# Attention scores as two packed fp32r products, and page loads shared between two queues

## The chip, the cores and the metric

The kernel runs on one core of a Trainium2 chip. A core has five engines that run side by side and meet at semaphores: TensorE (PE: matrix products from SBUF into PSUM), VectorE (DVE), ScalarE (ACT), GpSimd (POOL) and SyncE (SP), which here only issues DMAs. The metric is the device time of one execution in microseconds.

## The reference

The program is one inference step of a two-layer decoder for a prompt of 1024 tokens and, with the same weights, for 8 samples of one token each. Layer 0 mixes by a short convolution beside attention with a forget gate; layer 1 by a gated linear recurrence; both have an MLP behind them. Only the attention of layer 0 is touched here:

```python
def fox_attend(q, k, v, f_q, f_k, q_pos, k_pos):
    s = jnp.einsum('bqhd,bkhd->bhqk', q, k, preferred_element_type=jnp.float32)
    s = s + jnp.swapaxes(f_q, 1, 2)[..., :, None] - jnp.swapaxes(f_k, 1, 2)[..., None, :]
    s = jnp.where(k_pos[None, :] <= q_pos[:, None], s, -1e30)
    p = jax.nn.softmax(s, axis=-1)
    return jnp.einsum('bhqk,bkhd->bqhd', p.astype(v.dtype), v)
```

The prompt has 8 heads of 64 features and 1024 queries and keys, causal. Each of the 8 samples attends to 2048 cached rows in 16 pages of 128 rows, which stand anywhere in a pool (`cache_k[page_table]`, `cache_v[page_table]`, a page being 128 x 512 fp32, 256 KB), and to its own new row.

## The kernel before

Every engine has a program of its own, written out in order by hand; there is no scheduler. Most of the kernel is dense layers (`product`, `L855`): fp32 operands are split into a high part in fp32r and a low rest, and three fp32r products (high-high, high-low, low-high) of 128 x 128 weights by 344 columns are summed. The attention stage, from some 383 to 720 us in the trace of before, stands between the first layer's input projection and its output projection.

The stage is a loop over h = 0 to 7 (`head`, one for each engine), in which head h of the prompt is weighted and normed, head g = h + 1 is prepared, and sample h attends to its cached pages. For head g TensorE turns keys and queries from token rows to feature rows (`keys_turned`, `queries_turned`), ScalarE copies them from PSUM to `kT[g % 2]` and `qT[g % 2]` (`keys_kept`, `queries_kept`), and `scores` computes the scores with queries as rows, in 12 pieces of 128 queries by 128 to 512 keys. VectorE takes the maximum of each piece (`peak_of`), and then makes each query's shift (`shift`). For head h TensorE turns the shift into rows of `qT` (`shift_turned`, 16 small products, `L1123`, the first thing of a head), computes the scores again with keys as rows, in 12 pieces (`scores_turned`, `L1136`), ScalarE takes their exponents into `PT` (`exponent`, `L1582`), and `weighted` (`L1151`) multiplies these by the values. Score products are fp32: 64 features plus a row for the cumulated log forget value of the key (`negF`), and with keys as rows one more for the shift (`QS`). A piece on the diagonal gets a bf16 product of 128 columns that adds the mask.

A piece of 512 columns is a PSUM bank. `scores` go round three banks (`RING`), so piece p waits for the maximum of piece p - 3; `scores_turned` use two banks, so piece p waits for exponent p - 2. In TensorE's order, value product p stands behind score piece p + 1 and behind the score pieces of the next head given by `scores_at` (two each at p = 2 to 6, one at 7 and 8). ScalarE's order in a head is: two copies of the shift rows, the softmax denominator of head h - 1, two copies of keys, exponent 0, two copies of queries, exponents 1 to 11.

Sample h's cached keys come by pairs of pages, eight pairs, into seven slots (`kpages`, `L582`), are multiplied by the query on GpSimd (`L778`, `keys_multiplied`, for sample h + 1 during head h) and reduced on VectorE (`L1985`, `key_scores`). The values come into eight slots (`vpages`), and TensorE multiplies them by the sample's weights at the end of the head (`sequence_values`, `L1178`). All of these loads are issued by SyncE, in `load_pages`: for each page it reads the page's number from the table on the chip (`pt`) into a register, checks its bounds, and issues a DMA. SyncE's order is, for each h: eight pairs of keys, each when its slot is free, then the eight pairs of values of sample h + 1.

## Time and profile before

| | |
|---|---|
| runs of before | 2924.05, 2926.5, 2928.64 us; median 2926.5 |
| the profiled execution | 2922.55 us, of which the traced span is 2920.7 |
| TensorE busy | 2813.4 us, 96% of the span, granted clock 0.987 of full on average |
| VectorE, GpSimd, ScalarE busy | 1307.9, 883.9, 530.9 us |
| chain that ended last | 90% on TensorE; 69% in the dense layers' line 855 |
| lines of the attention's fp32 products | L1111, L1136 and L1151, 2% each of the chain; 74.1, 81.7 and 83.0 us busy |
| cached pages | 2 x 128 DMAs of 256 KB, median 3.0 to 3.1 us from issue to landing |

The busy time of an engine is the union of its instructions' spans; a matrix product's record includes its way through the array, so the distance between starts and not the duration of one says what it costs in a row of them. An fp32 product appears as two records. The chain follows the work back from the last instruction through what released each step. A stage lasts as long as its chain; an engine with gaps in the stage can still hold the others up at one place in it.

### The profile page before, as it was taken

What the parts mean: (1) busy time and instruction counts of PE and PEld (TensorE: products, weight loads), DVE (VectorE), ACT (ScalarE), POOL (GpSimd) and SP (SyncE); (2) the same over time, 40 slices, a digit from 0 to 9 for tenths busy, and PEclk for the clock granted to TensorE, in tenths of its full rate; (3) what the DMA queues carried; (4) which work ended last, traced back from release to release, by engine and by line L of the source; (5) the groups of instructions that cost most, each with busy time, mean ns of one, the idle gap of its engine ahead of it and who ended that gap; (6) DMA issues with size and microseconds to landing.
All of it is one profiled execution on the core that took longest, in us unless ns stands there. A gap on an engine that the chain in (4) does not pass through costs nothing.

```text
span 2920.7 us, 42681 instructions
## 1 busy us (share of the span) xinstructions
PE 2813.4 (96%) x16931; PEld 2498.8 (86%) x16931; DVE 1307.9 (45%) x2088; ACT 530.9 (18%) x829; POOL 883.9 (30%) x490
## 2 busy tenths in 40 slices
PE   5999989999999999999999999999899999999998
PEld 3899954445899999999999899954899999999998
DVE  3116755554354343444356303156454444434445
ACT  4200012323041010100101413134241010010100
POOL 2322235443222322333323322200324333243330
PEclk9999999999999999999999999999999999999999
DMA  7411267775512322223211322141301111111111
GB/s 313 123 44 37 59 202 234 217 213 152 210 37 101 101 73 90 84 82 107 66 37 44 103 63 103 51 147 55 118 30 56 45 44 46 41 50 38 55 43 58
DMA packets 208126, 275.37 MB, mean 94 GB/s; under 512 B 10742, under 2 KB 152713, under 8 KB 201068
## 3 DMA queue, kind: packets, MB, share of 16 engines
q1 hardware_dynamic: 204812, 255.89, 27.6%
q10 hardware_dynamic: 3024, 16.88, 1.5%
q8 instruction: 107, 1.75, 0.3%
q0 software_dynamic: 144, 0.52, 0.0%
q14 instruction: 39, 0.32, 0.0%
HBM read 245.24 MB, written 28.04 MB: 94 GB/s over the span
## 4 chain that ended last, share of the span: by engine, by line
PE 90%; DVE 4%; issue 2%; ACT 2%; SPq 1%; DMA 1%; POOL 0%; DVEq 0%; ACTq 0%
PE ps L855 69%; PE ps L873 4%; PE ps L841 2%; PE ps L1151 2%; PE ps L1136 2%; PE ps L1111 2%; PE ps L997 1%; PE ps L1178 1%; DVE xT L1856 1%; PE ps L1305 1%; PE ps L904 1%; PE ps L1294 1%; PE ps L1333 1%; PE ps L1312 1%; DMA ada_late<-in_w_ada_dram 1%
## 5 line engine op out<-in xcount | busy, mean ns | idle before, releaser
L756 POOL CAST whi<-stage 128x1024 fp32r<-128x1024 f32 x194 | 207.9, 1072 | 1770.5 <-PE ps L855 1298.5
L855 PE MATMUL ps<-hh,whi 128*128 128x344 f32 x2832 | 607.7, 323 | 5.7 <-issue 2.0
L855 PE MATMUL ps<-hl,whi 128*128 128x344 f32 x2832 | 601.6, 321 | 0.0
L855 PE MATMUL ps<-hh,wlo 128*128 128x344 f32 x2832 | 598.0, 319 | 0.0
L757 POOL TENSOR_TENSOR wlo<-stage,whi 128x1024 fp32r<-128x1024 f32 x194 | 519.4, 2677 | 15.5
L855 PEld LDWEIGHTS ps<-hh,whi 128*128 128x128 f32 x2832 | 474.4, 188 | 26.1 <-issue 24.6
L855 PEld LDWEIGHTS ps<-hl,whi 128*128 128x128 f32 x2832 | 479.5, 189 | 0.0
L855 PEld LDWEIGHTS ps<-hh,wlo 128*128 128x128 f32 x2832 | 472.1, 188 | 0.0
L855 PE MATMUL ps<-hid_hi,whi 128*128 128x344 f32 x1536 | 330.4, 323 | 10.7 <-DVE xT L1856 10.7
L855 PE MATMUL ps<-hid_lo,whi 128*128 128x344 f32 x1536 | 326.6, 321 | 0.0
L855 PE MATMUL ps<-hid_hi,wlo 128*128 128x344 f32 x1536 | 324.8, 320 | 0.0
L1877 DVE TENSOR_TENSOR tmp<-tmp 128x1032 f32<-128x1032 f32 x64 | 81.3, 1271 | 532.3 <-ACT tmp L1496 532.3
L855 PEld LDWEIGHTS ps<-hid_hi,whi 128*128 128x128 f32 x1536 | 254.9, 188 | 27.0 <-DVE xT L1856 17.0
L1496 ACT ACTIVATE tmp<-ps 128x1032 f32<-128x1032 f32 x64 | 66.2, 1034 | 1150.6 <-PE ps L855 1142.6
L855 PEld LDWEIGHTS ps<-hid_lo,whi 128*128 128x128 f32 x1536 | 258.0, 188 | 0.0
L855 PEld LDWEIGHTS ps<-hid_hi,wlo 128*128 128x128 f32 x1536 | 257.7, 189 | 0.0
L1856 DVE SCALAR_TENSOR_TENSOR xT<-ps,modT,xT 128x688 f32<-128x688 f32 x269 | 248.4, 924 | 0.0
L1842 DVE TENSOR_TENSOR t<-ps,modT 128x8 f32<-128x8 f32 x272 | 45.1, 166 | 347.9 <-PE ps L855 320.3
L778 POOL TENSOR_TENSOR kpages<-kpages,qbc 128x1024 f32<-128x1024 f32 x60 | 140.5, 2372 | 141.9 <-DMA kpages<-in_cache_k_dram 140.8
L1844 DVE SCALAR_TENSOR_TENSOR xT<-ps,modT,xT 128x336 f32<-128x336 f32 x272 | 152.1, 559 | 0.1
L1882 DVE TENSOR_TENSOR hid_lo<-tmp,hid_hi 128x1032 fp32r<-128x1032 f32 x64 | 106.6, 1665 | 41.9 <-ACT hid_hi L1498 38.6
L1843 DVE TENSOR_TENSOR xT<-xT,t 128x8 f32<-128x8 f32 x272 | 102.6, 377 | 9.3
(331 smaller groups left out, 2477.7 us busy)
## 6 DMA issues: line engine op xcount, KB each, us to landing
stage<-in_w_ff_dram SPq DMA_DIRECT2D x128, 512.0 KB, 3.9
kpages<-in_cache_k_dram SPq DMA_DIRECT2D x128, 256.0 KB, 3.1
vpages<-in_cache_v_dram SPq DMA_DIRECT2D x128, 256.0 KB, 3.0
ada_late<-in_w_ada_dram SPq DMA_DIRECT2D x32, 1024.0 KB, 5.2
stage<-in_w_in_even_dram SPq DMA_DIRECT2D x25, 512.0 KB, 3.9
stage<-in_w_in_odd_dram SPq DMA_DIRECT2D x25, 512.0 KB, 3.9
xstore<-xT ACTq DMA_DIRECT2D x2, 4128.0 KB, 12.6
xT<-xstore SPq DMA_DIRECT2D x2, 4128.0 KB, 12.5
```

Of the source, the lines that this page charges most:

```text
L756: link(pool.tensor_copy(whi[:, u.c % 4, :], stage[:, u.c % 2, :]))
L757: pool.tensor_tensor(wlo[:, u.c % 4, :], stage[:, u.c % 2, :], whi[:, u.c % 4, :].bitcast(F32), ALU.subtract).then_inc(w_split, 1)
L778: pool.tensor_tensor(kk, kk, qbc[:, b % 2, :].unsqueeze(1).to_broadcast([P, 2, 512]), ALU.mult).then_inc(k_mul, 1)
L841: return pe.transpose(out, in_, ident[0:k, 0:k])
L855: last = pe.matmul(ps[:, 3 * t.par + c, 0:CH], w, x[:, c * CH:(c + 1) * CH], start=(k == 0 and q == 0), stop=(k == n - 1 and q == 2))
L873: return pe.matmul(ps[:, 3 * ((t.c + j) % 2) + c, 0:CH], w, x[:, k, c * CH:(c + 1) * CH], start=(k == 0 and first), stop=(k == KT - 1 and ...
L1496: act.activation(thirds(tmp[:, j, :]), acc(tt.par), ACT.Relu).then_inc(acc_free[tt.par], 1)
L1843: tt(xT[:, f, 0:NS], xT[:, f, 0:NS], t8[:, :], ALU.add)
L1844: first = stt(out=xT[:, f, NS:CH], in0=ps[:, s, NS:CH], scalar=modT[:, l, m, NS:NC], in1=xT[:, f, NS:CH], op0=ALU.mult, op1=ALU.add)
L1856: stt(out=x2, in0=ps[:, s + 1:s + 3, 0:CH], scalar=modT[:, l, m, NS:NC], in1=x2, op0=ALU.mult, op1=ALU.add).then_inc(acc_free[t.par], 1)
L1877: tt(tmp[:, j, :], tmp[:, j, :], tmp[:, j, :], ALU.mult).then_inc(hid_squared, 1)
L1882: tt(hid[1][:, i.c % 2, j, :], tmp[:, j, :], hid[0][:, i.c % 2, j, :].bitcast(F32), ALU.subtract).then_inc(hid_ready, 1)
```

## The change

Four things, all in the attention stage.

1. Scores. `qT` and `kT` hold fp32r values, each the rounded high part, and there are four more buffers: `qhl` with the query's high part in rows 0 to 63 and its low rest in rows 64 to 127, and `klh` with the key's low rest in rows 0 to 63 and its high part in rows 64 to 127. A score piece is two fp32r products: high by high (with the rows for forget value and shift, each now as a high and a low row) and, over 128 rows at once, high by low plus low by high. The high parts in the new buffers are copied by ScalarE from `kT` and `qT` (four more copies a head), the low rests are made by VectorE from PSUM (`key_lows`, `query_lows`), and TensorE waits for both.
2. `PT` is a ring of three pieces instead of room for a head's 12, so exponent n waits for value product n - 3.
3. The two page numbers of a pair are read by one instruction, and not checked; instead VectorE clamps the page table once.
4. The cached values of samples 1 to 7 are issued by ScalarE, a pair each behind exponents 1 to 8. The semaphore `xt_done` also counts the low parts.

```diff
-        PT = at("PT", [P, NB * (NB + 1) // 2 * P], F32, B0)
-        qT = [at(f"qT{i}", [HD + 2, SEQ], F32, B0 + 18432 + 4096 * i) for i in range(2)]
-        kT = [at("kT0", [HD + 2, SEQ], F32, B0 + 26624), at("kT1", [HD + 2, SEQ], F32, W0 + 8192 + 4096 * KSLOTS)]
+        PT = at("PT", [P, 3, 512], F32, B0)
+        qT = [at(f"qT{i}", [HD + 4, SEQ], F32R, o) for i, o in enumerate((W0 + 4096, B0 + 6144))]
+        kT = [at(f"kT{i}", [HD + 4, SEQ], F32R, o) for i, o in enumerate((B0 + 10240, W0 + 8192 + 4096 * KSLOTS))]
+        qhl = [at(f"qhl{i}", [P, SEQ], F32R, B0 + 14336 + 4096 * i) for i in range(2)]
+        klh = [at(f"klh{i}", [P, SEQ], F32R, B0 + 22528 + 4096 * i) for i in range(2)]
...
             def load_pages(cache, slot, n, sem):
 
-                for q in range(2):
-                    page = sp.value_load(pt[0:1, 2 * n + q:2 * n + q + 1], min_val=0, max_val=cache_k.shape[0] - 1)
+                _, pages = nc.values_load_multi_w_load_instructions(
+                    pt[0:1, 2 * n:2 * n + 2], engines=[mybir.EngineType.SP], min_val=0, max_val=cache_k.shape[0] - 1,
+                    skip_runtime_bounds_check_because="the page table's copy on the chip is clamped to the cache's pages")
+                for q, page in enumerate(pages):
                     sp.dma_start(slot[:, q, :], cache[ds(page, 1), 0].rearrange("a p h d -> (a p) (h d)")).then_inc(sem, 16)
...
-                for j in range(8):
-                    load_values(h + 1, j)
+            sp.wait_ge(a_st, NP * (NH - 1))
             load_unit(V(U_OUT[0]), woe[:, :, 0:P])
...
             def queries_turned(g, c):
                 if c == 0 and g:
                     pe.wait_ge(a_q2, 2 * g)
                 if c == 1:
-                    pe.wait_ge(a_k, 2 * g + 1)
+                    pe.wait_ge(a_k, 4 * g + 1)
+                    pe.wait_ge(xt_done_or_lows, lows(4 * g + 1))
...
                 o = ps[:, RING[(4 + p) % 3], 0:w]
-                last = pe.matmul(o, qT[g % 2][0:HD + 1, i * P:(i + 1) * P], kT[g % 2][0:HD + 1, lo:lo + w],
-                                 start=True, stop=not diag)
+                pe.matmul(o, qT[g % 2][0:HD + 2, i * P:(i + 1) * P], kT[g % 2][0:HD + 2, lo:lo + w], start=True, stop=False)
+                last = pe.matmul(o, qhl[g % 2][:, i * P:(i + 1) * P], klh[g % 2][:, lo:lo + w], start=False, stop=not diag)
...
-                last = pe.matmul(o, kT[h % 2][0:HD + 2, j * P:(j + 1) * P], qT[h % 2][0:HD + 2, lo:lo + w],
-                                 start=True, stop=not diag)
+                pe.matmul(o, kT[h % 2][0:HD + 4, j * P:(j + 1) * P], qT[h % 2][0:HD + 4, lo:lo + w], start=True, stop=False)
+                last = pe.matmul(o, klh[h % 2][:, j * P:(j + 1) * P], qhl[h % 2][:, lo:lo + w], start=False, stop=not diag)
...
+                act.activation(kT[g % 2][0:HD + 2, cols], ps[0:HD + 2, RING[c], :], ACT.Copy).then_inc(a_k, 1)
+                act.wait_ge(a_k, 4 * g + 2 * c + 1)
+                act.activation(klh[g % 2][HD:P, cols], kT[g % 2][0:HD, cols].bitcast(F32), ACT.Copy).then_inc(a_k, 1)
...
-                o = key_at[j] + lo - j * P
-                act.activation(PT[:, o:o + w], ps[:, 4 + p % 2, 0:w], ACT.Exp).then_inc(a_p, 1)
+                n = NP * h + p
+                if n >= 3:
+                    act.wait_ge(a_av, n - 2)
+                act.activation(PT[:, n % 3, 0:w], ps[:, 4 + p % 2, 0:w], ACT.Exp).then_inc(a_p, 1)
+
+            def load_values(b, j):
+                act.wait_ge(v_used, 4 * (b - 1) + j // 2 + 1)
+                n = 8 * b + j
+                _, pages = nc.values_load_multi_w_load_instructions(
...
+                for q, page in enumerate(pages):
+                    act.dma_start(vpages[:, j, q, :], cache_v[ds(page, 1), 0].rearrange("a p h d -> (a p) (h d)")
+                                  ).then_inc(first_or_values[j], 16)
...
                 for p in range(1, NP):
                     exponent(h, p)
+                    if h and p <= 8:
+                        load_values(h, p - 1)
...
+                link(dve.tensor_scalar(QS[:, :, 2], peak[:, :], -1.0, None, ALU.mult))
+                stt(out=QS[:, :, 3], in0=peak[:, :], scalar=-1.0, in1=QS[:, :, 2].bitcast(F32), op0=ALU.mult, op1=ALU.subtract
+                    ).then_inc(a_shift, 1)
+
+            def key_lows(g, c):
+                dve.wait_ge(a_k, 4 * g + 2 * c + 1)
+                cols = slice(512 * c, 512 * c + 512)
+                tt(klh[g % 2][0:HD, cols], ps[0:HD, RING[c], :], kT[g % 2][0:HD, cols].bitcast(F32), ALU.subtract
+                   ).then_inc(xt_done_or_lows, 1)
...
                 if more:
                     key_scores(8 * g)
+                    for c in range(2):
+                        key_lows(g, c)
+                    for c in range(2):
+                        query_lows(g, c)
                 sequence_top(h)
```

ScalarE near a head's start, before: from the shift rows of head 1 to exponent 2 (`qT`, `kT` are the operands in SBUF, `rden` the denominators, `PT` the exponents).

```order
L1575 ACTIVATE qT_140<-ps 2x512 [waits a_again] x2
L1592 ACTIVATE rden<-ps 64x512 [waits a_av]
L1594 ACTIVATE rden<-rden 64x512 [waits a_lnd]
L1567 ACTIVATE kT_141<-ps 65x512 [waits a_tk] x2
L1582 ACTIVATE PT<-ps 128x512 [waits a_st]
L1571 ACTIVATE qT_139<-ps 64x512 [waits a_tq] x2
L1582 ACTIVATE PT<-ps 128x512 [waits a_st]
L1582 ACTIVATE PT<-ps 128x384 [waits a_st]
```

The same place in the changed kernel, from the second copy of keys to the first pair of value pages.

```order
L1574 ACTIVATE klh_146<-kT_142 64x512 [waits a_k]
L1594 ACTIVATE PT<-ps 128x512 [waits a_av,a_st]
L1579 ACTIVATE qT_140<-ps 64x512 [waits a_tq]
L1581 ACTIVATE qhl_144<-qT_140 64x512 [waits a_q]
L1579 ACTIVATE qT_140<-ps 64x512 [waits a_tq]
L1581 ACTIVATE qhl_144<-qT_140 64x512 [waits a_q]
L1594 ACTIVATE PT<-ps 128x512 [waits a_av,a_st]
L1599 TENSOR_LOAD pt [waits v_used]
L1603 ISA
L1603 DMA vpages<-in_cache_v_dram 128x512
```

Each copy to `kT` and `qT` has a second, dependent copy behind it, ahead of exponents 0 and 1, and behind exponent 1 stand the load of page numbers and the DMAs.

TensorE in the middle of a head, before: score pieces of head h (`L1136`) and h + 1 (`L1111`), masks (`L1139`, `L1114`), a value product (`L1151`).

```order
L1136 MATMUL ps<-qT_139,kT_141 128x512 [waits a_p]
L1111 MATMUL ps<-kT_142,qT_140 128x512 [waits a_max]
L1111 MATMUL ps<-kT_142,qT_140 128x128 [waits a_max]
L1114 MATMUL ps<-negb,identb 128x128
L1151 MATMUL ps<-PT,Vp 128x256 [waits a_p]
```

The same place now.

```order
L1142 MATMUL ps<-qT_139,kT_141 128x512 [waits a_p]
L1143 MATMUL ps<-qhl_143,klh_145 128x512
L1117 MATMUL ps<-kT_142,qT_140 128x512 [waits a_max]
L1118 MATMUL ps<-klh_146,qhl_144 128x512
L1117 MATMUL ps<-kT_142,qT_140 128x128 [waits a_max]
L1118 MATMUL ps<-klh_146,qhl_144 128x128
L1120 MATMUL ps<-negb,identb 128x128
L1157 MATMUL ps<-PT,Vp 128x256 [waits a_p]
```

The order of pieces and their waits is the same; a piece is two instructions instead of one (which the trace shows as two records for fp32).

VectorE at the start of the same head, now (`small` and `peaks` are the maxima of sample and prompt).

```order
L2010 TENSOR_REDUCE sc<-kpages 128x16 [waits k_mul]
L2182 TENSOR_TENSOR klh_146<-ps,kT_142 64x512 [waits a_k] x2
L2188 TENSOR_TENSOR qhl_144<-ps,qT_140 64x512 [waits a_q] x2
L2136 TENSOR_REDUCE small<-ps 8x1 [waits d_tops_turned]
L2137 TENSOR_SCALAR small<-ident,small 8x8 [waits dve_link]
L2168 TENSOR_REDUCE peaks<-ps 128x1 [waits a_s] x2
```

The four instructions in rows two and three are new; the others stood in this order before.

## Rows read from the trace of the kernel before

**Rows 1.** Window: length, busy (count) of PE, PEld, DVE, ACT, POOL; clock, DMA share, GB/s.
```profile
470.00:510.00 40.00, 39.20 (x183) 18.69 (x181) 20.65 (x36) 11.64 (x23) 19.57 (x9) 1.00 0.81 235
```

**Rows 2.** Chain of waits: start us, duration us, engine, tile, line, count.
```profile
450.09 1.84 PE ps L1123 x16
...
490.55 1.84 PE ps L1123 x16
...
498.60 0.59 ACT kT L1567
...
501.39 1.07 ACT qT L1571 x2
...
503.09 1.10 PE ps L1151 x2
...
515.41 0.12 PE ps L1169 x2
...
522.70 0.91 PE ps L1151 x2
...
531.00 1.07 PE ps L1123 x9
...
692.84 1.84 PE ps L1123 x16
...
718.44 0.02 issue
```

**Rows 3.** Chain, score pieces of 512, 384, 256 and 128 columns.
```profile
504.30 0.86 PE ps L1136 x2
...
480.57 0.65 PE ps L1136 x2
...
483.15 0.43 PE ps L1136 x2
...
472.35 0.22 PE ps L1136 x2
```

**Rows 4.** Window of line 855 alone (fp32r, 344 columns): PE and PEld busy (count).
```profile
1000.00:1010.00 10.00, 9.09 (x58) 8.81 (x57) 1.00 0.26 77
```

**Rows 5.** Timeline of ScalarE: start us, us, engine, line, operation, tiles.
```profile
493.03 0.59 ACT L1592 ACTIVATE rden<-ps 64x512 f32<-64x512 f32 x1
493.65 0.63 ACT L1594 ACTIVATE rden<-rden 64x512 f32<-64x512 f32 x1
```

**Rows 6.** VectorE: a window; then by line busy, mean ns | idle before; one timeline row.
```profile
504.33:523.43 19.10, 19.10 (x68) 9.98 (x67) 15.59 (x24) 5.00 (x10) 10.03 (x5) 1.00 0.82 236
...
L2140 DVE TENSOR_REDUCE peaks<-ps 128x1 f32<-128x512 f32 (+3 forms) x12 | 6.5, 554 | 3.4 <-PE ps L1111 2.1 <-PE ps L1114 1.3
L1985 DVE TENSOR_REDUCE sc<-kpages 128x16 f32<-128x1024 f32 x5 | 6.0, 1209 | 0.0
L2108 DVE TENSOR_REDUCE small<-ps 8x1 f32<-8x128 f32 x1 | 0.3, 279 | 7.8 <-PE ps L841 7.8
...
523.67 2.34 DVE L2147 TENSOR_SCALAR QS<-peak 128x8 f32<-128x8 f32 x1
```

**Rows 7.** Queues of SyncE and ScalarE: issue, a timeline row, then by line min/median/max ns.
```profile
490.52 17.78 SPq L582 DMA_DIRECT2D vpages<-in_cache_v_dram  x16
...
L581 SPq TENSOR_LOAD <-pt x53: 262/268/279, 479.9 to 543.9; - x53
L582 SPq DMA_DIRECT2D vpages<-in_cache_v_dram x28: 332/333/1016, 490.5 to 544.6; - x28
L611 SPq DMA_DIRECT2D out_dram<-in_state_conv_dram x1: 5601/5601/5601, 415.2 to 415.2; - x1
...
L1667 ACTq DMA_DIRECT2D rstore<-qe x4: 343/352/382, 1737.6 to 1811.7; - x4
```

**Rows 8.** Window with stores and page loads together, columns as in rows 1.
```profile
410.00:415.00 5.00, 5.00 (x27) 2.20 (x24) 0.38 (x1) 1.18 (x2) 0.00 (x0) 0.85 1.02 377
```

**Rows 9.** Timeline of TensorE, the shift of head 0, with the wait ahead of it.
```profile
408.57 3.31 PE L1123 MATMUL ps<-ident,QS 128*2 128x128 f32 x16 [7.31 <-DVE QS L2147]
```

More of the change, by code:

```diff
@@ L162, in build @@
         lft = put("lft", [P, NB + 1, NH])
-        negF = put("negF", [P, NB, NH])
-        QS = put("QS", [P, NB, 2])
+        negF = put("negF", [P, NB, NH, 2], F32R)
+        QS = put("QS", [P, NB, 4], F32R)
         prevT = put("prevT", [P, 4, 16])
@@ L448, in multiplied, with lows @@
             return n // 2 + 1 if n < PAGES // 2 else n - 3
-        key_at = [sum(SEQ - m * P for m in range(j)) for j in range(NB)]
+        def lows(n):
+            return KT + n
         def all_read(eng, t):
@@ L603, in _ @@
             for j in range(8):
-                load_values(0, j)
+                load_first_values(j)
             sp.wait_ge(qk_scaled, 2 * NB)
@@ L990, in _ @@
                                 xin[:, b, k * P:(k + 1) * P])
-                last.then_inc(xt_done, 1)
+                last.then_inc(xt_done_or_lows, 1)
             pe.wait_ge(setup_dve, 3)
@@ L1085, in keys_turned @@
                     turn(o[0:HD, :], QK[:, 1, b, g * HD:(g + 1) * HD])
-                    last = pe.matmul(o[HD:HD + 1, :], negF[:, b, g:g + 1], ident[:, :], start=True, stop=True)
+                    last = pe.matmul(o[HD:HD + 2, :], negF[:, b, g, :].bitcast(F32), ident[:, :], start=True, stop=True)
                 last.then_inc(a_tk, 1)
@@ L1580, in exponent @@
                 act.wait_ge(a_st, NP * h + p + 1)
-                o = key_at[j] + lo - j * P
-                act.activation(PT[:, o:o + w], ps[:, 4 + p % 2, 0:w], ACT.Exp).then_inc(a_p, 1)
+                n = NP * h + p
[6 more added lines that the diff above has]
+                _, pages = nc.values_load_multi_w_load_instructions(
+                    pt[0:1, 2 * n:2 * n + 2], engines=[mybir.EngineType.Activation], min_val=0, max_val=cache_k.shape[0] - 1,
+                    skip_runtime_bounds_check_because="the page table's copy on the chip is clamped to the cache's pages")
+                for q, page in enumerate(pages):
+                    act.dma_start(vpages[:, j, q, :], cache_v[ds(page, 1), 0].rearrange("a p h d -> (a p) (h d)")
+                                  ).then_inc(first_or_values[j], 16)
             def denominator(h, c):
@@ L2188, in head @@
                 sequence_masked(h)
+            for c in range(2):
+                key_lows(0, c)
+            for c in range(2):
+                query_lows(0, c)
             dve.wait_ge(prep_pe, PE_STEP["u_turned"])
```

54 lines of the change are left out of this document (31 added, 23 removed).

## Prediction

> **What bounds the kernel now.** I read the windows of the attention stage first, then the chain of waits through one head, then the durations by line, and last the queues of SyncE and ScalarE. The windows show TensorE busy 39.2 of 40 us at the full clock, while VectorE is busy 20.7, ScalarE 11.6 and GpSimd 19.6 [rows 1]. The chain gives the period of a head as the distance between two shift products (`L1123`): 490.55 - 450.09 = 40.46 us. Head 7 starts at 692.84, so heads 1 to 6 take (692.84 - 450.09) / 6 = 40.46 us each; head 0 starts at 408.57 [rows 9] and takes 41.5, the last head, which prepares no other, ends at 718.44 and takes 25.6 [rows 2]. Inside a head the chain is TensorE, except near its start, where it passes twice through ScalarE: a copy of keys and then an exponent (from 498.60), and two copies of queries and then an exponent (from 501.39), after which the second value product starts at 503.09 [rows 2]. So what shortens the score products shortens the head, as long as neither ScalarE's two passages nor VectorE takes over.
>
> **The score products.** Each fp32 score product stands as two MATMUL records: a piece of 512 columns takes 0.86 us, of 384 0.65, of 256 0.43, of 128 0.22 [rows 3]. The new form is two fp32r products per piece. The trace has none of 512 columns, but 58 of 344 columns fill 9.09 us, 0.157 us each [rows 4]. In proportion to columns, a product of 512 takes 0.233 us and a pair 0.47, say 0.46 as part of the 0.157 will not grow. I save 0.40 us on a piece of 512, 0.30 on 384, 0.19 on 256. For 128 columns the two ends are 2 x 0.058 = 0.12 us in proportion, and 2 x 0.157 = 0.31 if loading the 128 weights is the floor; the row that is nearest, the fp32 pair at 0.22, makes me take 0.17. The ends for all sizes: no gain at all (a product as long as an fp32 record, 0.43) and 0.42 per large piece. A head has 12 pieces of queries and 12 of keys, each set six of 512 and two each of 384, 256 and 128: 12 x 0.40 + 4 x 0.30 + 4 x 0.19 + 4 x 0.05 = 6.96 us of TensorE time per head.
> By the Trainium skill's page TensorE: Matmul & The Clock Gate (Back-to-back issue gap), a product of N columns takes N/2.4 ns and some 2.5 ns; a product of 344 would be 0.146 us where the row has 0.157, and a pair of 512 would be 0.43 us, 0.03 below my value and 0.4 us more gain per head. The measured row decides.
>
> **ScalarE's copies at the head's start.** This takes a part back. Key copies: the second key copy starts 0.02 us after TensorE, takes 0.59, and exponent 0 starts 0.49 after it (independent instructions overlap by 0.1: two query copies fill 1.07 instead of 2 x 0.59). Now a second copy of the same block waits for the first to end and lies ahead of exponent 0. Two dependent ScalarE instructions of this size start 0.62 us apart [rows 5]. The keys come 0.40 earlier (the first score piece), the exponent 0.62 later: the first value product starts 0.2 us later than before, and the second score piece's gain is lost in that wait. Query copies: two independent ones take 1.07 us; now copy, dependent copy, copy, dependent copy: exponent 1 starts 0.62 + 0.49 + 0.62 + 0.49 = 2.22 us after the first copy's start rather than 2 x 0.49 = 0.98, +1.25. The second value product starts (before at 503.09) 0.2 + 1.3 = 1.5 us later, at 504.6. VectorE's low parts (four of 64 x 512, 0.7 us each if they go by columns like the peaks, 0.554 for 384 in the mean) stand where it sits idle for 7.8 us [rows 6]; the wait of query turns for the first of them is met, as it follows one key reduction (1.21) and the first copy is done 2 us before. They cost nothing unless the key reduction ahead of them is late.
>
> **The rest of a head.** From 503.09 to 531.00 TensorE spent 27.91 us. Nine score pieces of keys (4 x 0.40 + 0.30 + 2 x 0.19 + 2 x 0.05 = 2.38) and the 12 of queries (3.48) take 5.86 off: 22.05. VectorE now comes close. From 504.33 to 523.43 it did 15.6 us of work, with 3.4 idle for score pieces [rows 6]; TensorE's share of that stretch falls from 19.1 by 2.2 (keys) and 3.5 to 13.4. TensorE came to the spread of the sums (`L1169`) 12.3 us after the start of its second value product [rows 2]; less 1.0 (four key pieces) and 2.0 (eight of queries) that is 9.3. VectorE starts 504.33 - 503.09 = 1.24 later and has until the sums two top instructions (0.9), six peaks of 0.554 (3.3), three key reductions of 1.21 (3.6), shifting and sums (0.65): 9.7. The difference is 0.4 us; with the way through the semaphores I add 0.5. After that TensorE's waits for free banks are met, and the sequence's weights are ready about when the first cached values are multiplied. The shift (`L2147`, 2.34 us here) gets a second small instruction; between the last peak and the next head lie eight products and the cached values, over 5 us [rows 2, 6]. Head: 504.6 + 22.05 + 0.5 = 527.1, from 490.55 that is 36.6 us, 3.9 less.
>
> **Pages.** On SyncE a page takes 17.78 / 16 = 1.11 us of issue: a load of 0.27, a DMA of 0.33, and register steps, a check and gaps between [rows 7]. Sixteen value and sixteen key pages are 35.5 us of the 40.46, so SyncE itself would have been near the bound at 36.6; that is what moving the values away buys, and it needs no gain of its own. A pair now is one load, and two DMAs each with a register step, without the check: some 0.30 + 2 x 0.52 = 1.34 us (an estimate from that 1.11: load and check were 0.59 of it). ScalarE's own DMAs elsewhere take 0.34 to 0.38 us of issue [rows 7]. Eight pairs, 10.7 us per head, stand in ScalarE's order behind exponents 1 to 8. Behind each waits the next exponent, for which the next value product waits. From exponent 1 to 8 TensorE needed 19.6 us (503.09 to 522.70, second to ninth value product [rows 2]), now 19.6 - 5.7 + 0.5 = 14.4: seven steps of 2.06 us, against 1.4 for dispatching an exponent and a pair: hidden, with 0.6 us to spare. Even if the load waited for the running exponent (0.60) it would be 1.94. In the last head a step of TensorE is only some 1.3 us, so there ScalarE leads with 8 x 1.4 us, and of the 3.5 us that the products save 0.8 remain. The value slots were freed a head earlier, so that wait costs nothing.
> The values then come in 14 us, together with five pairs of keys: 13 x 0.524 MB = 6.8 MB. The engines moved 377 GB/s between 410 and 415 us, and 235 at a share of 0.81 in heads (290 at full) [rows 1, 8]. At 377 this is 18 us and the last pair is there 1 to 2 us before its product; at 290 it is 23.5, some 4.5 us too late. I take 377, since the 235 were set by the issue of 1.11 us per page.
> The Trainium skill's page DMA: Bandwidth & Descriptors (Issuing engines are not separate DMA queues) says that DMAs of several engines share the same 16 and only the issuing time is saved; its page Perfetto Trace Analysis (DMA Instruction, HWDGE) has a lock on the descriptor generator that the queues share, so that each of ScalarE's DMAs might wait for one of SyncE's. No row here shows two queues issuing densely together. By that rule, with the 0.33 us of a row for each wait, a step would be 1.4 + 2 x 0.33 = 2.06 us, just what TensorE leaves; past it lies rival (1).
>
> **Outside heads 1 to 6.** Before head 0 the scores start 1.5 us later for ScalarE's four added copies, VectorE gets back 1 to 1.5 of the gaps it had between peaks, and TensorE's wait of 7.3 us for the shift stays [rows 9]: 0, with +1.5 as an end. Head 0 has no value pages on ScalarE; it saves 3.9 and, as keys are issued in 1.34 instead of 2.2 us, some of the 1.1 us by which it was longer: 4.5. The clamp of the page table, the second negF and the ring of three PT buffers (a product three pieces back) are 0.2 to 0.4 us beside other work: 0.
> Sum: 6 x 3.9 + 4.5 + 0.8 = 28.7, of which I take 28. The profiled execution took 2922.55 us (span 2920.7), the median is 4 above it; 2922.5 - 28 = 2894.5 there, 2898.5 as the median.
>
> **Rivals.** (1) Slower: ScalarE's queue leads. Place: the two DMA issues between exponents 1 and 8. For it: on SyncE the same instruction took up to 1.02 us in this stage, and 5.6 behind the stores of 2 MB each [rows 7]. Against: its median is 0.33. It decides from a step of 2.06 us, and makes the head longer than before from (14.4 + 3.9) / 7 = 2.6 us, that is 0.93 us per DMA. At 1.02 each, a step is 2.75: heads of 41.6 (+1.1 x 6), the last +8, less 4.5 for head 0: 2937. (2) Values land late: at 290 GB/s a head is 36.6 + 4.5 = 41.1, and all but head 0's gain is gone: 2925 to 2930, no change. (3) VectorE or ScalarE bind more than I see (a small instruction as long as `L2147`'s 2.34 us in a worse place; low parts behind a late key page): 2 us more in seven heads, 2912. (4) Nothing takes back: 7 x 7 + 3.5 + 1 = 53 us, 2873. (5) fp32r pairs of full fp32 length: the copies remain, 7 x 1.9 - 1 more, 2938; 58 products at 0.157 speak against.
>
> **Chances.** Forecast 0.64 (2882 to 2912), (3) 0.13, (4) 0.05, (2) 0.06, (1) 0.10, (5) 0.02. The range 2878 to 2925 takes in the forecast, (3), the milder half of (2) and leaves out about 0.2. What differs by less than 0.2% (5.9 us) can't be told from no change. Faster: 0.64 + 0.12 + 0.05 + 0.01 = 0.82; same 0.06; slower 0.12.
>
> **What would show it.** Distance between shift products 36 to 37 us instead of 40.46; a pair of 512 columns at 0.46; the start of the second value product 14 us after the shift; TensorE waiting some 2 us there and 0.5 at the sums; ScalarE's DMAs at 0.33 to 0.4 us each; no wait for value pages at `L1178`. I am wrong if the heads stay at 40 us: then the cached values' product waits for DMA (2) or value products wait for exponents at every piece (1).

## The result and the profile after

The changed kernel took 2917.7 us (median of 19 runs, 2907.3 to 2930.0) beside 2927.1 for the kernel before (19 runs, 2923.2 to 2934.4): a ratio of 0.9966, 95% interval 0.9955 to 0.9977. It is faster, by 9.4 us, where 28 were forecast. Its times spread over 23 us; those of before over 11.

Its first profiled execution is the longest of the 19, 2930.0 us; a second one took 2905.4, below all 19. The two stand at both ends of what one program does, and most of what separates them (23.5 of 24.6 us) lies in heads 1 to 6. No profile shows an execution near the median. The window of heads 1 to 6 of either, first the long one (columns as in [rows 1]; clock, DMA share and GB/s last):

```profile
449.08:701.92 252.84, 227.50 (x1099) 118.91 (x1098) 148.43 (x243) 86.14 (x162) 103.69 (x47) 0.87 0.59 198
```

```profile
449.19:678.57 229.38, 204.45 (x1099) 110.84 (x1098) 148.21 (x243) 86.16 (x162) 103.67 (x46) 0.98 0.65 219
```

Before, six heads took 242.75 us at clock 1.00 [rows 1, 2]. TensorE was busy 39.20 of 40 us then; now it is busy 204 of 229, and the mean granted clock is 0.98 or 0.87: of its two levels it was at 1.2 GHz for about 2 x 0.13 = 26% of the long window (66 us) and 4% of the short one (9 us). The chain of waits of the long profile, with the starts of heads 1, 2, 3, 4, 6 and 7 and the DMAs between them (start, length, what), answers to [rows 2]:

```profile
449.15 1.84 PE ps L1129 x16
...
491.33 3.51 PE ps L1129 x16
...
525.68 8.35 DMA vpages<-in_cache_v_dram
...
536.21 1.84 PE ps L1129 x16
...
565.18 8.77 DMA vpages<-in_cache_v_dram
...
576.12 1.84 PE ps L1129 x16
...
658.37 3.51 PE ps L1129 x16
...
701.99 1.85 PE ps L1129 x16
```

Heads last 42.2, 44.9, 39.9, 40.3, 41.9 and 43.6 us instead of 40.46. Two things are new in the chain: loads of value pages ahead of a head's end, and two shifts, those of heads 2 and 6, whose 16 products took 3.51 us where they took 1.84 [rows 2], which is the same work at 1.2 GHz. Both lie in a long stretch at 1.2 GHz that starts inside a wait for value pages. The first (columns as above):

```profile
486.50:510.50 24.00, 22.04 (x74) 9.24 (x75) 4.44 (x7) 6.32 (x11) 17.18 (x8) 0.50 0.16 58
```

TensorE waited 2.74 us for pages there, until 487.55. The second starts in a wait of 2.52 us and runs from 654 to 677. The two make some 48 of the 66 us.

The short profile shows the head without disturbance. Head 2 of it, TensorE's timeline (start, length, line, shapes; in brackets the idle time and its releaser), down to the next head's shift:

```profile
488.25 1.91 PE L1129 MATMUL ps<-ident,QS 128*4 128x128 f32 x16
...
498.01 1.10 PE L1157 MATMUL ps<-PT,Vp 128*128 128x512 f32 x2 [1.38 <-ACT PT L1594]
...
502.61 1.10 PE L1157 MATMUL ps<-PT,Vp 128*128 128x512 f32 x2 [2.20 <-ACT PT L1594]
...
508.71 0.40 PE L1117 MATMUL ps<-kT,qT 66*128 66x512 f32 x1
508.94 0.40 PE L1118 MATMUL ps<-klh,qhl 128*128 128x512 f32 x1
509.18 0.22 PE L1117 MATMUL ps<-kT,qT 66*128 66x128 f32 x1
...
510.13 0.48 PE L1117 MATMUL ps<-kT,qT 66*128 66x512 f32 x1
510.45 0.39 PE L1118 MATMUL ps<-klh,qhl 128*128 128x512 f32 x1
510.68 0.28 PE L1117 MATMUL ps<-kT,qT 66*128 66x256 f32 x1
...
523.60 1.06 PE L1182 MATMUL ps<-vpages,PBx 128*32 128x512 f32 x8 [0.41 <-DMA vpages<-in_cache_v_dram]
...
525.57 0.60 PE L1129 MATMUL ps<-ident,QS 128*4 128x128 f32 x4
```

A pair of 512 columns fills 509.18 - 508.71 = 0.47 us behind another fp32r product and 0.55 behind a diagonal's bf16 product (0.32 to the second, not 0.23), against 0.86 [rows 3]. TensorE waits 1.38 and 2.20 us for exponents 0 and 1, and 0.41 for the last value pages. ScalarE in the same head (ACTq is its queue), answering to [rows 5, 7]:

```profile
500.21 0.63 ACT L1581 ACTIVATE qhl<-qT 64x512 fp32r<-64x512 f32 x1
...
501.89 0.57 ACT L1594 ACTIVATE PT<-ps 128x512 f32<-128x512 f32 x1
502.10 0.83 ACTq L1603 DMA_DIRECT2D vpages<-in_cache_v_dram  x2
503.04 0.49 ACT L1594 ACTIVATE PT<-ps 128x384 f32<-128x384 f32 x1 [0.58 <-issue]
503.71 0.84 ACTq L1603 DMA_DIRECT2D vpages<-in_cache_v_dram  x2
...
515.20 0.88 ACTq L1603 DMA_DIRECT2D vpages<-in_cache_v_dram  x2
```

And what the loads' instructions took over six heads (min/median/max ns), with the time from issue to landing in us:

```profile
L1599 ACTq TENSOR_LOAD <-pt x48: 486/497/689, 463.1 to 691.5; - x48
```

```profile
L1603 ACTq DMA_DIRECT2D vpages<-in_cache_v_dram x96: 339/340/827, 464.0 to 692.7; - x96
...
DMA to landing us min/median/max: 2.6/4.2/10.1
```

A DMA's issue costs what was forecast (0.34 us); the load of the page numbers takes 0.50 where 0.30 was. The eight pairs are issued from 502.1 to 516.1, the last of them lands at 523.5, and TensorE was there at 523.2. From the first issue to that landing the engines moved 320 GB/s, and in the first 4 us, while pages are issued one pair in 1.6 us, 160:

```profile
502.10:523.50 21.40, 20.58 (x107) 11.75 (x107) 19.03 (x29) 6.48 (x14) 11.13 (x6) 1.00 0.90 320
...
502.00:506.00 4.00, 3.39 (x18) 2.39 (x18) 2.08 (x6) 1.55 (x3) 2.54 (x2) 1.00 0.57 160
```

The DMA stretch 475 to 490 of the same profile (DMA busy tenths, GB/s, then queue SP and queue ACT with packets, MB and share):

```profile
DMA  9999999999999999999999999978995979499951
GB/s 415 404 399 399 366 361 388 404 388 415 344 344 371 377 366 393 393 399 404 393 393 404 388 399 377 213 126 284 393 437 202 218 158 213 175 388 393 339 197 55
...
q1 hardware_dynamic: 1725, 3.14, 62.0%
q10 hardware_dynamic: 1053, 1.90, 33.9%
```

Both queues together move some 390 GB/s while they are full, here the first 9 us of the 15.

### The profile page after: what moved, and what is told of

It reads as the page before. It is cut to its first block, busy times and chain, and to the rows that moved or that the text cites. A ratio compares the mean times of both kernels' runs of the same rounds, so it can differ in the third digit from the quotient of the medians.

```text
span 2928.3 us, 42220 instructions
## 1 busy us (share of the span) xinstructions
PE 2793.0 (95%) x16931; PEld 2504.5 (86%) x16931; DVE 1327.9 (45%) x2130; ACT 551.9 (19%) x861; POOL 882.6 (30%) x490
## 4 chain that ended last, share of the span: by engine, by line
PE 88%; DVE 5%; ACT 2%; DMA 2%; issue 2%; ACTq 0%; SPq 0%; DVEq 0%
PE ps L859 68%; PE ps L877 4%; PE ps L845 3%; PE ps L1157 2%; DMA vpages<-in_cache_v_dram 2%; PE ps L1001 1%; DVE xT L1880 1%; PE ps L1090 1%; PE ps L1309 1%; PE ps L908 1%; PE ps L1337 1%; PE ps L1298 1%; PE ps L1129 1%; PE ps L1316 1%; PE ps L1182 1%
## 5 line engine op out<-in xcount | busy, mean ns | idle before, releaser
L1906 DVE TENSOR_TENSOR hid_lo<-tmp,hid_hi 128x1032 fp32r<-128x1032 f32 x64 | 106.5, 1664 | 41.9 <-ACT hid_hi L1502 38.6
L1157 PE MATMUL ps<-PT,Vp 128*128 128x512 f32 (+3 forms) x192 | 88.6, 544 | 24.7 <-ACT PT L1594 24.1
```

Source lines behind the costliest of these rows:

```text
L1157: last = pe.matmul(ps[:, 2 + c, lo - 512 * c:512], Vp[:, j, odd:odd + 2, :].rearrange("p e d -> p (e d)"), PT[:, (NP * h + p) % 3, 0:w], s ...
L1906: tt(hid[1][:, i.c % 2, j, :], tmp[:, j, :], hid[0][:, i.c % 2, j, :].bitcast(F32), ALU.subtract).then_inc(hid_ready, 1)
```

## The experiments

The theories, as the expectations name them. L: value pages land late, and the clock falls from that wait. I: their issue holds ScalarE up. K: the clock falls without them, in the pauses that the shorter products leave. C: ScalarE's order at the head's start makes these pauses. K2, K's second form: the clock falls because TensorE stands in these pauses. P: VectorE and GpSimd share a port. "Behind the heads" is from the end of the last sequence's product to the end of the span. Each run is compared with the kernel before on the same chip (2926.8 to 2928.4 there).

**Without the value pages of samples 1 to 7.** Those samples are weighted with stale pages.

```diff
-                    if h and p <= 8:
-                        load_values(h, p - 1)
-                    pe.wait_ge(first_or_values[j], 16 + 32 * (b + 1))
+                    pe.wait_ge(first_or_values[j], 16 + 32)
```

> The changed kernel without the value pages of samples 1 to 7: ScalarE issues none of them and TensorE waits only for the first sample's (samples 1 to 7 are weighted with stale pages). Theory L (late landing: TensorE stands at the value products of a head, and the clock falls to 1.2 GHz from that): heads 1 to 6 take 36 to 37 us each instead of 39.9 to 44.9, the granted clock stays at 1.0 in them as in head 0, and the time is 25 to 32 us under the kernel before, some 2897. Rival I (the cost is the pages' issue on ScalarE): the same time, since the issue is gone too. Rival K (the shorter packed products alone leave TensorE too idle, and the clock falls with no page waited for): heads stay at 39 us or more with stretches at 1.2 GHz, and the time stays within 15 us of the kernel before.

2905.4 us, ratio 0.9927 (0.9913 to 0.9940). Heads 37.8 to 39.6 us. Its window of heads 1 to 6:

```profile
450.78:682.28 231.50, 211.42 (x1100) 115.58 (x1100) 144.51 (x244) 85.55 (x162) 103.46 (x46) 0.94 0.35 108
```

That is between the forecasts of L (2897) and K (within 15 us of the kernel before). L alone is refuted: no page is waited for and the clock is still at 0.94. In head 3, from 528.53, it falls behind the two waits for exponents 0 and 1:

```profile
528.53:542.60 14.07, 10.78 (x67) 5.95 (x66) 6.21 (x11) 8.11 (x14) 7.03 (x3) 1.00 0.46 132
542.70:546.00 3.30, 3.12 (x7) 1.72 (x7) 0.50 (x2) 0.41 (x2) 0.00 (x0) 0.50 0.00 0
```

Every head of this run has such a stretch, 10 to 15 us after its start. K holds for a part.

**A sixteenth of the bytes.** The issues stay, each page's first 32 of 512 columns are moved.

```diff
-                    act.dma_start(vpages[:, j, q, :], cache_v[...].rearrange("a p h d -> (a p) (h d)")
+                    act.dma_start(vpages[:, j, q, 0:32], cache_v[...].rearrange("a p h d -> (a p) (h d)")[:, 0:32]
```

> The changed kernel with every value page issued as before by ScalarE in its place, but only 32 of the page's 512 columns moved (samples 1 to 7; a sixteenth of the bytes; the rest of the tile is stale). Theory L (the bytes land late): the pages land within 2 to 3 us of their issue, nothing waits at the value products, heads 36.5 to 37.5 us at clock 1.0, the time 22 to 30 us under the kernel before. Rival I (the issue delays ScalarE's exponents, and TensorE behind them): as the changed kernel as it stands, heads of 40 us or more, 10 us under the kernel before. Rival K (clock without waits): the same as in the run without values, short of L.

2907.4 us, ratio 0.9930 (0.9916 to 0.9943). So bytes cost 10.3 of the changed kernel's time. The issue makes 2 us more than the run without pages, which the intervals can't part: in the profiles the last head is 4.1 us longer with it (29.2 and 25.1), but heads 1 to 6 are 3.3 shorter and what lies behind the heads 5.0. Heads 1 to 6:

```profile
451.20:679.45 228.25, 209.99 (x1099) 114.36 (x1098) 146.60 (x244) 86.27 (x162) 103.34 (x47) 0.95 0.40 116
```

**SyncE issues the values again**, by pairs, behind the key pages.

```diff
+                for j in range(8):
+                    load_values(h + 1, j)      # SyncE
-                    if h and p <= 8:
-                        load_values(h, p - 1)  # ScalarE
```

> The changed kernel with the value pages issued by SyncE again, behind the key pages of the same head and by pairs; the packed scores stay. SyncE has 32 pages in a head; at the 17.8 us that 16 pages took before less half of the register loads it issues them in about 31 us of a 36.6 us head. Theory L: what matters is when they are issued; keys come first on the queue, so the values of a head are issued no earlier than with ScalarE, and it is 0 to 15 us slower than the changed kernel, about 2917 to 2930. Rival I: ScalarE is free of the issue, heads get to 37 us and the time falls to 2900 or under.

2908.3 us, ratio 0.9934 (0.9921 to 0.9948): between the two ranges (I 2900 or under, L 2917 or over). I had the order wrong: SyncE has issued the next head's keys by the end of a head, and sends the values in the first 12 us of a head, not in its second half. All of them land in time:

```profile
448.91:679.94 231.03, 211.46 (x1099) 115.54 (x1099) 144.48 (x243) 85.57 (x162) 103.62 (x46) 0.94 0.66 217
```

217 GB/s here and 108 without the values, in the same time: bytes that come early cost nothing.

**Value pages earlier on ScalarE.**

```diff
+                    load_values(h, 4)          # behind the second denominator
...
+                if h:                          # behind exponent 0
+                    load_values(h, 5)
+                    load_values(h, 6)
...
-                    if h and p <= 8:
-                        load_values(h, p - 1)
+                    if h and p == 1:
+                        load_values(h, 7)
...
+                if more:                       # behind exponent 11
+                    for j in range(4):
+                        load_values(g, j)
```

> The changed kernel with the same value pages issued by ScalarE earlier: pairs 0 to 3 of the next sample behind the last exponent piece of a head (ScalarE idles 5 us there), pair 4 behind the second denominator, 5 and 6 behind the first exponent piece of the next head, 7 behind its second. Theory L: all land 8 us or more before their product, no wait there and clock 1.0; heads of 36.5 to 37.5 us, the time 22 to 30 us under the kernel before, some 2900. Rival I: the issue costs ScalarE as much wherever it stands, and earlier it stands ahead of the key and query copies that TensorE waits for: no better than the changed kernel, 2915 to 2925. Rival K: clock falls anyway, no gain over the changed kernel of more than 5 us.

2917.6 us, ratio 0.9971 (0.9961 to 0.9982): as the changed kernel. No page was waited for, but the four pairs at a head's end hold ScalarE until the slots are free and beyond. TensorE waits for the shift's copy 1.5 us in head 1 and 0.2 to 0.5 in four others, and the mean clock of heads 1 to 6 is 0.93. The time is in rival I's range (2915 to 2925), and in K's (no gain over 5 us); the trace shows rival I's place, but whether that is all of it stays open. ScalarE, then TensorE:

```profile
443.19 6.43 ACTq L1603 DMA_DIRECT2D vpages<-in_cache_v_dram  x8
449.67 1.07 ACT L1585 ACTIVATE qT<-ps 4x512 fp32r<-4x512 f32 x2 [7.07 <-PE ps L1129]
```

```profile
450.31 0.50 PE L1142 MATMUL ps<-qT,kT 68*128 68x512 f32 x1 [1.46 <-ACT qT L1585]
```

**The page changes alone**, on the kernel before.

```diff
+                _, pages = nc.values_load_multi_w_load_instructions(pt[0:1, 2 * n:2 * n + 2], ...)
...
-                for j in range(8):
-                    load_values(h + 1, j)      # SyncE
...
+                    if h and p <= 8:
+                        load_values(h, p - 1)  # ScalarE
                 last = pe.matmul(o, qT[g % 2][0:HD + 1, ...], kT[g % 2][0:HD + 1, ...])   # fp32, as before
```

> The kernel before (fp32 scores, its large tile for the exponents) with the page changes alone: page numbers by pairs, and samples 1 to 7's value pages issued by ScalarE behind its exponent pieces 1 to 8. The issue stands about 4 us earlier against the value products than in the changed kernel, since heads take 40.46 us and not 36. Theory L (late landing decides): the last pages land before their product, heads stay at 40.5 us, same time as before within 3 us. Rival I (the issue on ScalarE costs): exponents run late by 0.3 us or more eight times in a head, heads 41 to 43 us, 5 to 20 us slower than before.

2922.9 us, ratio 0.9982 (0.9973 to 0.9991), and not the 5 to 20 us slower of rival I. Heads 1 to 6 are the old ones to 0.01 us, at full clock:

```profile
453.27:696.03 242.76, 237.98 (x1100) 114.15 (x1099) 125.20 (x210) 70.60 (x138) 102.68 (x47) 1.00 0.61 204
```

The other stages of its profile are not the same: head 0 takes 45.3 us instead of 41.5 (TensorE waits 2.0 for VectorE's product of 6.85 us beside ten GpSimd products, and the clock is at 0.91 instead of 0.97), the last head 28.8 instead of 27.5, with ScalarE's issue in it, and what lies behind the heads is 3.6 us shorter. SyncE is done with pages earlier and sends the modulation weights of the next layer part sooner: in the kernel before TensorE waited for them 3.7 us (the profiles' line L997, here of before), in the changed one 1.4.

```profile
  DMA ada_late<-in_w_ada_dram: 3.7, 2
```

**TensorE's pauses filled**, with SyncE's values: work that nobody reads, in place of waiting.

```diff
+                if p < 2:
+                    for i in range((6, 9)[p]):
+                        pe.matmul(ps[:, 2 + c, 0:P], ident[:, :], ident[:, :], start=True, stop=True)
                 pe.wait_ge(a_p, NP * h + p + 1)
```

> The run with SyncE's values, with TensorE's waits for exponent pieces 0 and 1 filled: 6 and 9 products of the identity with itself (fp32, 128 columns, 0.22 us each, 1.3 and 1.9 us) into the accumulator that the piece's own product then starts anew. It tells the clock from the waits: the waits stay as long, only TensorE's activity changes. Theory K2 (the clock falls because TensorE stands there): no stretch at 1.2 GHz in heads 1 to 6, each head 36.0 to 36.6 us instead of 37.7 to 39.6, time 2893 to 2900. Rival (the clock falls for something else): stretches stay, time 2908 to 2912 (each filler ends 0 to 0.3 us late).

2898.7 us, ratio 0.9902 (0.9888 to 0.9916), 9.6 under the run with SyncE's values, though TensorE does more. Heads 36.51 to 36.55 us:

```profile
448.40:667.61 219.21, 218.97 (x1280) 129.37 (x1279) 142.20 (x243) 85.56 (x162) 103.62 (x46) 1.00 0.70 229
```

That is K's second form shown: nothing but TensorE's activity in the pauses is different, and the clock stays at 2.4 GHz. Over heads 1 to 6 that is 11.8 us (231.0 to 219.2); the last head, where nothing was to be gained, is 2.4 longer.

**The same fillers in the changed kernel**, ScalarE issuing the values (edit as above).

> The changed kernel as it stands, ScalarE issuing the values, with the same 6 and 9 filler products in TensorE's two waits for exponents 0 and 1. With the changed kernel (2917.7), the run with SyncE's values (2908.3) and that with SyncE's values and fillers (2898.7) it closes the square. If late pages and the pauses at a head's start act apart: 2917.7 - 9.6, 2908 within 3. If the late pages alone let the clock fall (their waits stand behind 20 us of work): 2914 or more. If the pauses at a head's start are what the page waits need to let it fall: 2902 or under.

2916.7 us, ratio 0.9956 (0.9943 to 0.9970): not told from the changed kernel. Heads 1 to 6 took 233.2 us at clock 0.98, with 7.6 us of waits for value pages:

```profile
448.00:681.23 233.23, 225.23 (x1280) 130.63 (x1279) 143.91 (x243) 86.13 (x162) 104.27 (x47) 0.98 0.63 215
```

```profile
  DMA vpages<-in_cache_v_dram: 7.6, 5
```

Of the three forecasts that is the second (2914 or more): the page waits let the clock fall by themselves. It is at 1.2 GHz from some 37 us after the start of head 1, and from 38 after that of head 5, for 7 and 3 us, across the next head's start, and nowhere else in heads 1 to 6. Late pages take back what the clock gives: the two losses don't add. How much of this run's time is something else stays open, as its profile is also 6.6 us longer behind the heads than the long profile of the changed kernel.

**Exponents 0 and 1 earlier.** Theory C, with ScalarE's values.

```diff
+                exponent(h, 0)
                 if more:
                     keys_kept(g, 0)
                     keys_kept(g, 1)
-                exponent(h, 0)
+                exponent(h, 1)
...
-                    exponent(h, p)
+                    if p > 1:
+                        exponent(h, p)
```

> The changed kernel with exponent pieces 0 and 1 of a head moved in ScalarE's order: piece 0 ahead of the four key copies, piece 1 ahead of the four query copies, where ScalarE idles 1.8 and 1.7 us (run without values). Theory C (TensorE's two waits of 1.4 and 2.2 us for these pieces are ScalarE's order, and the clock falls behind them): both waits go, up to 3.5 us a head, and with them most stretches at 1.2 GHz; but the value pages are issued where they were and are needed 3 us earlier, so part comes back at the value products: 2895 to 2912. Rival (the copies themselves bind: what goes at the exponents comes back at the scores' wait for the query copies): no change against the changed kernel, 2917 within 4.

2912.6 us, ratio 0.9956 (0.9942 to 0.9969): between C's range and the rival's, and its interval overlaps with the changed kernel's, so by the time alone it settles nothing. The waits for exponents 0 and 1 fell from 3.6 to between 0.5 and 1.0 us, and a wait for value pages of 1.6 to 3.3 us took their place in five of six heads, 12.4 us in all. Head 0 has a new wait too, 5.5 us for VectorE, as in the next run:

```profile
  DMA vpages<-in_cache_v_dram: 12.4, 5
```

**The same, with SyncE's values.**

> The same new places of exponent pieces 0 and 1, and the value pages issued by SyncE as in the run with SyncE's values (2908.25). Theory C: heads 1 to 6 lose the two waits (3.5 us) and one stretch at 1.2 GHz (1.7 us of a stretch of 3.4): 33 to 35 us instead of 37.7 to 39.6, so 8 heads by 4 us: 2876 to 2888. Rival (copies bind): 2904 to 2910. Rival K (TensorE's own idle share lets the clock fall in any case): half of it, 2890 to 2900.

2884.5 us, ratio 0.9851 (0.9837 to 0.9865). Heads of 33.2 and 34.3 us in turn, at full clock:

```profile
453.49:655.88 202.39, 198.90 (x1099) 107.67 (x1099) 150.28 (x240) 85.24 (x162) 103.22 (x46) 1.00 0.75 244
```

The copies don't bind; their place ahead of two exponents did. Only head 0 got longer, 43.0 us, with 5.4 of waiting for VectorE and the clock at 0.86. TensorE, then VectorE in head 0 and in head 1, then GpSimd:

```profile
445.20 1.94 PE L1186 MATMUL ps<-vpages,PBx 128*32 128x512 f32 x8 [5.43 <-DVE PBx L2157]
```

```profile
437.08 8.06 DVE L2157 TENSOR_TENSOR PBx<-PBx,small 128x136 f32<-128x136 f32 x1
...
477.83 0.30 DVE L2157 TENSOR_TENSOR PBx<-PBx,small 128x136 f32<-128x136 f32 x1
```

```profile
419.40 25.59 POOL L786 TENSOR_TENSOR kpages<-kpages,qbc 128x1024 f32<-128x1024 f32 x11 [21.67 <-DMA kpages<-in_cache_k_dram]
```

VectorE's product ends at 445.14, 0.15 us behind the end of GpSimd's block (444.99). So it does in the two other runs with a long block: 443.20 and 443.04 with ScalarE's values and the new order, 445.43 and 445.27 with the page changes alone.

**Key pages 10 to 14 ahead of the stores.**

```diff
+            for n in range(KSLOTS + 3, KSLOTS + 8):
+                load_keys(n)
             sp.wait_ge(qk_scaled, 2 * NB)
             ...                                # nine stores
-            for n in range(KSLOTS + 3, KSLOTS + 8):
-                load_keys(n)
```

> The run with SyncE's values and the two exponents moved, with the key pages 10 to 14 issued by SyncE ahead of the nine stores at the start of head 0 and not behind them. There head 0 took 43.0 us, with a wait of 5.4 us for VectorE's product for the weights of the first sample (128x136, two SBUF inputs), which took 8.06 us beside 11 key products of GpSimd without a pause and 0.30 us in other heads. Theory P (a port that the two engines share: VectorE's product starts only when GpSimd pauses): GpSimd begins its key products some 10 us earlier and has no block of 11; the product takes 0.3 to 2.3 us, head 0 takes 36 to 38 us, time 2877 to 2880. Rival (the DMA's keys set it, not the port): GpSimd's block only starts earlier or stays, head 0 within 2 us of 43.0, time 2884.

2882.5 us, ratio 0.9847 (0.9833 to 0.9860). GpSimd works in shorter blocks, VectorE's product takes 1.92 us, and head 0 takes 34.2 at a clock of 0.94:

```profile
440.48 1.92 DVE L2157 TENSOR_TENSOR PBx<-PBx,small 128x136 f32<-128x136 f32 x1
```

The place and the product's time are as the port theory has them; head 0 is shorter than its 36 to 38 us, 8.8 less than above where the wait was 5.4, with the clock higher too. But head 0 starts 4.6 us later (415.1 instead of 410.5), so 4 us stay in the profiles and 2.0 in the medians, less than the two intervals can part, and the time misses the 2877 to 2880 expected. A shared port is the explanation that fits; no run rules out another.

**The last sample's pages split** between the queues, on top of that.

```diff
-                for j in range(8):
+                for j in range(8 if h < NH - 2 else 4):
                     load_values(h + 1, j)      # SyncE
+                    if h == NH - 1 and p in (1, 2, 3, 4):
+                        load_values_act(h, p + 3)      # ScalarE
```

> The run above, with the value pages of the last sample split: pairs 0 to 3 by SyncE, 4 to 7 by ScalarE behind its exponent pieces 1 to 4 of the last head, which has no key or query copies. SyncE gets to the output projection's weights and the late modulation weights 6 us earlier: theory: the wait of 1.9 us for a late modulation weight after the heads, and the stretch of 3.4 us at 1.2 GHz behind it, go (they are absent in the changed kernel): 3 to 4 us less than the run above. Rival: the four pairs on ScalarE hold up its exponents or land late in the last head: the same or up to 3 us slower than the run above.

2878.5 us, ratio 0.9831 (0.9817 to 0.9844), the fastest: 49.9 us under the kernel before and 39 under the changed one. It is 4.0 us under the run above, as expected, though the intervals overlap. The wait for modulation weights behind the heads is down to 0.4 us, from 3.5.

**The changed kernel once more.**

> The changed kernel unaltered, profiled once more, since its first profiled execution (2930.0 us) was the longest of 19 and 12 us over their median of 2917.7. Theory L with the clock: the value pages are issued and land at the same places (15 to 28 us into a head, 8 to 10 us each at the end), TensorE waits for them in most heads, but less time is at 1.2 GHz: heads of 38 to 41 us, the profiled execution within 6 us of 2917.7. If the first profile shows the rule and not the tail, heads are 40 to 45 us again.

2914.5 us (5 runs), ratio 0.9951 (0.9932 to 0.9971), and the profile shown above. Heads of 37.3 to 39.3 us, shorter than I expected, and an execution 12.3 us under 2917.7 where I expected one within 6: the first profile was one tail, this is the other.

## Why the prediction was wrong

The direction was right and the mechanism of the gain was right to a few tenths; the time was 19 us too low, because one term was mis-sized and one missing.

- **Score products.** A pair was taken at 0.46 and measures 0.47 to 0.55. The stretch from the second value product to the next shift was put at 527.1 - 504.6 = 22.5 us; it is 22.55 without page waits (525.57 - 502.61 - 0.41). Right.
- **ScalarE's copies.** The second value product was forecast 14.05 us after the shift and comes at 14.36 (502.61 - 488.25). Right within 0.3. I counted what this costs in time and stopped there; that it makes two pauses of 1.4 and 2.2 us in an engine that had one of 0.6 was the start of the second failure.
- **A head of 36.6 us** is what remains once pages are early and the clock is kept: 36.5 in the run with fillers. That this run's 2898.7 us is the forecast of 2898.5 is in part luck: its profile is only 21.7 us under that of before, since its head 0 starts 2.7 us later and 3.3 more go by behind the heads, where I had nothing, and the last head gains nothing; the rest of the 28 is that the profile of before was 4.5 under its median and this one 2.2 over. VectorE's 0.5 at the sums shows as 0.50 us of waiting of TensorE's weight load, with the products ahead of it still running; rival (3) did not happen.
- **Step that failed first: the pages' bytes.** "At 377 this is 18 us and the last pair is there 1 to 2 us before its product ... I take 377." The bytes were right (6.84 MB in head 2 of the short profile), the rate over the whole stretch was not: the engines reach 350 to 395 GB/s only once pages have piled up, and from the first issue to the last landing it is 320 and 21.4 us. That is 3.4 us more than 18, where the margin was 1 to 2. The pages are issued from 13.9 us into the head, share the engines with key pages (12 of those beside the 16 value pages), and the last ones take 7.8 us there and up to 10.1 in the long profile. They come 0.4 to 1.2 us late in the short profile and up to 2.7 in the long one. Rival (2) was the right place with the wrong size. Removing the bytes gives back 10.3 us, earlier issue by SyncE 9.4.
- **Step that was missing: TensorE's clock.** Before, heads ran at 1.00 [rows 1], and I took this as given, with no reason, for an engine that would now be idle some 4 us in 37. The shift products alone went from 1.84 to 3.51 us in two heads. In the long profile 66 us of heads 1 to 6 at 1.2 GHz can cost up to half, 33 us, and the window is indeed 252.84 - 219.21 = 33.6 us longer than that of the filled run, page waits included. With pages out of the way the clock costs 9.6 us (2908.3 to 2898.7).
- 9.4 + 9.6 = 19.0 us is what the forecast lacked, with the luck above in it: SyncE's issue and then the fillers lead from 2917.7 to 2898.7. Taken in the other order the fillers give 1.1 and the pages 18.0, since a TensorE that is faster only waits longer for a page.
- **Rival (1), ScalarE's queue.** Median DMA issue 0.34 us and a step of 503.71 - 502.10 = 1.61: forecast 1.4, and under the 2.06 from which it would have decided (2.6 for a head longer than before). In the last head it did bind, as forecast, but more: 28.8 and 29.0 us against 27.5 (all three to the end of the last sequence's product), where I had -0.8; without the issues it is 25.1 to 25.3. ScalarE's DMAs show no sign of waiting for SyncE's: 0.34 us here, while SyncE issues key pages, and 0.35 where they were issued before [rows 7]. The lock on the shared descriptor generator that the Trainium skill's page Perfetto Trace Analysis (DMA Instruction, HWDGE) has did not cost anything that these medians show.
- **Head 0** was put at -4.5 and measured -4.2 and -2.7. **Before it** I had 0 (end +1.5); it starts 1.8 and 3.3 us later in the two profiles. There VectorE's low parts, which I had at nothing, hold up TensorE's first score pieces by 2.6 and 2.3 us; in the long profile the clock from 392 us to head 0 is at 0.56, where it was 0.88. No run separates the two. **Behind the heads** I had nothing and the two profiles show 4.1 and 3.1 us less (SyncE is free earlier). Short profile (before head 0, head 0, heads 1 to 6, last head, behind): +1.8 - 2.7 - 13.4 + 1.3 - 4.1 = -17.1 us, from 2922.55 to 2905.4.
- **The pages themselves** gave nothing inside heads 1 to 6 with fp32 scores, and with fp32r scores SyncE alone, by pairs, is faster than the change. What I had written, that moving them "needs no gain of its own", took it for harmless; it moved the issue from a head's first 18 us to the 14 us that begin 14 us into it.

## What to carry to other kernels

When an edit takes work from a TensorE that is busy all the time, list the pauses that it leaves and read the granted clock of the stretch before and after: here pauses of 1.4 and 2.2 us a head cost 2 us more a head in clock (11.8 over six), a page wait of 2.7 us stood at the start of 24 us at 1.2 GHz, and gains downstream vanish into that. A load moved to another queue must be placed by when its bytes are needed and what else is in flight, not by what its issue costs. If an engine copies for later use and another waits for a short instruction behind the copies, put the short one first: that order was worth 24 us here with SyncE issuing (with ScalarE issuing 5, not told from nothing), more than the packed products and the pairs of pages gave without it (19 us, SyncE issuing).

## What the runs showed that was not expected

- The same program had TensorE at a mean clock of 0.98 or 0.87 over six heads and took 229 or 253 us for them. Its times spread over 23 us in 19 executions, those of the kernel before, at full clock in these heads, over 11 in as many.
- 15 products a head that compute nothing made the kernel with SyncE's values 9.6 us faster.
- VectorE's product of 128x136 with two inputs in SBUF took 0.30 us with GpSimd idle and 8.06 within a block of 11 GpSimd products without a pause. The Trainium skill's page SBUF — State Buffer (SBUF: two separate sides) has the two engines hold a shared port by turns, each for a whole instruction. The trace agrees in kind, but a GpSimd product took 25.59 / 11 = 2.33 us, so VectorE waited over more than three of them and not one, until the block was over. In the changed kernel, with a block of five, it took 1.78 us and was through after one.
- Reading two page numbers into registers took 0.50 us on ScalarE (median of 48), where one took 0.27 on SyncE [rows 7].
